# A tuned two-block transformer kernel: the second feed-forward's up projection as block products with seven multiplications

## The chip, the cores and the metric

One core of a Trainium2 chip runs the whole program in one launch. The metric is the device time of that launch in microseconds. The engines meant below are TensorE (PE), VectorE (DVE), ScalarE (ACT), GpSimd (POOL) and SyncE (SP), which here only issues DMAs.

## The reference

Two transformer blocks over 1024 positions of width 1024, one after the other, in float32. The change touches the feed-forward of the second block:

```
u   = rms_norm_2(h, norm_mlp_pre)                # (1024 positions, 1024)
hid = square(relu(u @ w_up))                     # w_up: (1024, 4096)
m   = hid @ w_down                               # w_down: (4096, 1024)
h   = h + rms_norm_2(m, norm_mlp_post)
```

Everything else (the mixers of both blocks and the first feed-forward) is computed as before.

## The kernel before, in words

Activations lie with channels on the partitions and positions along the row: eight tiles of 128 channels by 1024 positions. Every large product is made of float32r matmuls of 128x128 weights on 128x512 positions. To keep float32 accuracy each operand is split into a high part and a low remainder, and three matmuls make one product: high by high, high by low, low by high (L1320 to L1322, in `mm`).

A weight panel is 128x1024 (512 KB). SP loads it into one of two raw buffers (`wraw`, `load`, L2949). ACT copies it with rounding into the high half of one of four slots (`whl`, NW = 4; the ACT `split`, L2408 is the helper's line), POOL subtracts to get the low half (the POOL `split`, L2847). A panel of w_up (`f2u`) covers 128 hidden channels and all 1024 input channels: 8 input tiles x 3 matmuls x 2 halves of the positions = 48 matmuls, in two PSUM tiles of 24. A panel of w_down (`f2d`) covers four hidden tiles and two output tiles, again 48 matmuls, in four PSUM tiles of 12.

The second feed-forward takes 32 f2u panels and 8 chunks of 4 f2d panels, and alternates: after six up panels, four down panels, four up panels, and so on (`ffn`, `ffn_order`). The last chunk's first half of positions is finished for all outputs before its second half, so that its panels come twice. For an up panel ACT evicts the two PSUM tiles with a Relu into `rl`, DVE squares the 128x1024 (`rl<-rl`), ACT writes the high half and POOL the low half of the hidden tile (`hid`); three of the first six low halves are made on DVE. Hidden tiles stay on the chip. For a down tile DVE adds the PSUM tile into `y` (`y<-y,ps`).

The order of the work is one list of steps, written by a planner (`Plan`, `plan.seq`); each engine walks that list and takes the steps that it has code for. So the queues are in order, and a step that waits holds everything that the same engine has behind it. Waits are on semaphores that `mark` and `done` name: `hi` and `lo` for the halves of a panel, `gemm` for a PSUM tile.

## Time and profile before

| | |
|---|---|
| device time, three runs | 2922.83, 2915.71, 2922.82 us (median 2922.82) |
| profiled execution, span | 2914.0 us (the page gives no other time of its own for it) |
| PE busy | 2752.9 us, 94% of the span |
| DVE, ACT, POOL busy | 1347.0, 871.3, 887.3 us |
| second feed-forward, last 700 us of the span | PE busy in all of it from 2250 to 2860 us |
| DMA | 246.47 MB, mean 85 GB/s |

The page gives the busy time of each engine, the chain of work that ended last, the costliest groups of instructions and the DMA issues. A row of a timeline has the start and the duration of an instruction in microseconds, its engine, its line, what it writes and reads, and in brackets how long its engine had been idle and who released it. A matmul's printed duration overlaps with the next one's, so that the pace of PE is read from starts. Where work on DVE, ACT, POOL or SP lies beside PE's, only its lateness counts.

### The profile page before, as it was taken

Reading aid. Unit: us, or ns where it says so; the run is one execution under the profiler, and the core shown is the slowest. Engines: PE = TensorE matmul, PEld = TensorE weight load, DVE = VectorE, ACT = ScalarE, POOL = GpSimd, SP = SyncE. Lnnn points to the kernel's source line nnn. Section 1 sums busy time; section 2 is a strip of 40 time slices with the busy share of each in tenths; the row PEclk is TensorE's granted clock in tenths of the full one; section 3 lists DMA queues with packets and bytes.
Section 4 is the critical chain, followed back from the end, with each engine's and each line's share of the span. In section 5 each row is a group of like instructions: output and inputs, shape, how many; then the busy total and the mean of one; then the engine's idle time right before and its main releaser. Section 6 shows DMA issues by size and latency. Waiting matters only on the chain.

```text
span 2914.0 us, 30872 instructions
## 1 busy us (share of the span) xinstructions
PE 2752.9 (94%) x12774; PEld 2145.0 (74%) x12774; DVE 1347.0 (46%) x1666; ACT 871.3 (30%) x1306; POOL 887.3 (30%) x410
## 2 busy tenths in 40 slices
PE   6888898799999999979999999999999999999997
PEld 3656666678888888767777777677677888888885
DVE  5646668775435453565757522322566212111116
ACT  4313563432212121234454221111344111222112
POOL 1422124243333342344211111111245333333234
PEclk8999999899999999989999999999999999999998
DMA  6453246211111111223112211111323111111113
GB/s 233 175 139 100 75 169 254 101 58 51 51 44 51 51 44 49 101 82 130 44 65 102 65 65 54 64 52 48 130 87 112 55 51 51 44 51 44 51 51 137
DMA packets 86571, 246.47 MB, mean 85 GB/s; under 512 B 10784, under 2 KB 25632, under 8 KB 86432
## 3 DMA queue, kind: packets, MB, share of 16 engines
q1 hardware_dynamic: 78400, 219.77, 22.1%
q10 hardware_dynamic: 4608, 14.92, 1.3%
q0 software_dynamic: 3424, 9.81, 0.9%
q8 instruction: 101, 1.65, 0.2%
q14 instruction: 38, 0.31, 0.0%
HBM read 207.40 MB, written 37.07 MB: 84 GB/s over the span
## 4 chain that ended last, share of the span: by engine, by line
PE 82%; DVE 10%; ACT 3%; issue 2%; DMA 2%; POOL 1%; SPq 0%; ACTq 0%; POOLq 0%; DVEq 0%
PE ps L1320 24%; PE ps L1322 23%; PE ps L1321 23%; PE pc L1667 3%; DVE x L1721 1%; PE pss L1617 1%; PE ps L1480 1%; PE ps L1534 1%; DMA adaw<-in_w_ada 1%; DVE pad L1691 1%; DVE pad L1685 1%; ACT act L2408 1%; PE ps L1499 1%; PE pss L1467 1%; POOL whl L2847 1%
## 5 line engine op out<-in xcount | busy, mean ns | idle before, releaser
L2847 POOL TENSOR_TENSOR whl<-wraw,whl 128x1024 fp32r<-128x1024 f32 (+1 forms) x247 | 645.2, 2614 | 1590.7 <-ACT whl L2408 1590.6
L1320 PE MATMUL ps<-act,whl 128*128 128x512 f32 x2464 | 998.2, 405 | 49.9 <-DVE act L1685 18.0
L1322 PE MATMUL ps<-act,whl 128*128 128x512 f32 x2464 | 974.0, 395 | 0.0
L1321 PE MATMUL ps<-act,whl 128*128 128x512 f32 x2464 | 973.9, 395 | 0.0
L1320 PEld LDWEIGHTS ps<-act,whl 128*128 128x128 f32 x2464 | 469.3, 190 | 183.2 <-issue 69.5
L1321 PEld LDWEIGHTS ps<-act,whl 128*128 128x128 f32 x2464 | 469.7, 191 | 105.5 <-issue 8.2
L1322 PEld LDWEIGHTS ps<-act,whl 128*128 128x128 f32 x2464 | 468.8, 190 | 103.3
L2408 ACT ACTIVATE whl<-wraw 128x1024 fp32r<-128x1024 f32 (+1 forms) x247 | 256.5, 1039 | 446.1 <-PE ps L1322 388.8
L1320 PE MATMUL ps<-hid,whl 128*128 128x512 f32 x864 | 340.4, 394 | 3.8 <-POOL hid L2847 2.1
L1322 PE MATMUL ps<-hid,whl 128*128 128x512 f32 x864 | 337.7, 391 | 0.0
L1321 PE MATMUL ps<-hid,whl 128*128 128x512 f32 x864 | 337.5, 391 | 0.0
L1685 DVE TENSOR_TENSOR y<-y,ps 128x512 f32<-128x512 f32 x176 | 120.4, 687 | 302.0 <-PE ps L1322 301.6
L1320 PEld LDWEIGHTS ps<-hid,whl 128*128 128x128 f32 x864 | 162.5, 188 | 39.5 <-POOL hid L2847 2.9
L1322 PEld LDWEIGHTS ps<-hid,whl 128*128 128x128 f32 x864 | 162.3, 188 | 36.4
L1321 PEld LDWEIGHTS ps<-hid,whl 128*128 128x128 f32 x864 | 162.4, 188 | 35.0 <-issue 0.5
L1685 DVE TENSOR_TENSOR rl<-rl 128x1024 f32<-128x1024 f32 x32 | 44.1, 1378 | 278.1 <-ACT rl L2408 278.1
L2408 ACT ACTIVATE sgm<-ps 128x512 f32<-128x512 f32 x46 | 27.5, 598 | 294.3 <-PE ps L1322 285.9
L1685 DVE TENSOR_TENSOR sgm<-sgm,pc 128x512 f32<-128x512 f32 x48 | 32.7, 682 | 156.3 <-PE pc L1667 156.1
L1667 PE MATMUL pc<-hz,wb 128*128 128x512 f32 x224 | 102.2, 595 | 0.4
L1691 DVE SCALAR_TENSOR_TENSOR cv<-pad,par,cv 128x1024 f32<-128x1024 f32 x44 | 100.0, 2273 | 1.6
L1691 DVE SCALAR_TENSOR_TENSOR pad<-pad,par 128x1024 f32<-128x1024 f32 x44 | 100.0, 2273 | 1.6
L2408 ACT ACTIVATE rl<-ps 128x512 f32<-128x512 f32 x61 | 36.4, 597 | 214.2 <-PE ps L1322 214.2
(312 smaller groups left out, 2471.6 us busy)
## 6 DMA issues: line engine op xcount, KB each, us to landing
wraw<-in_w_in SPq DMA_DIRECT2D x63, 512.0 KB, 3.3
wraw<-in_f1u SPq DMA_DIRECT2D x47, 512.0 KB, 3.2
wraw<-in_f2d SPq DMA_DIRECT2D x36, 512.0 KB, 3.2
wraw<-in_f2u SPq DMA_DIRECT2D x35, 512.0 KB, 3.2
wraw<-in_w_out SPq DMA_DIRECT2D x32, 512.0 KB, 3.3
x<-in_w_ada SPq DMA_DIRECT2D x32, 512.0 KB, 6.1
xs<-y SPq DMA_DIRECT2D x24, 512.0 KB, 7.4
x<-in_xT ACTq DMA_DIRECT2D x16, 512.0 KB, 9.4
```

The lines of the kernel that those rows point to most:

```text
L1320: pe.matmul(PSB[g.bank][:, :], hi, src[:, 0, k, c], start=e == 0, stop=False)
L1321: pe.matmul(PSB[g.bank][:, :], hi, src[:, 1, k, c], start=False, stop=False)
L1322: m = pe.matmul(PSB[g.bank][:, :], lo, src[:, 0, k, c], start=False, stop=e == len(ks) - 1)
L1467: pe.matmul(PSS[:, g, 0:hi - lo], qT[pr, i, n * 128:n * 128 + 128], kT[pr, kc], start=True, stop=True).then_inc(*mark("att", "score", u, g))
L1480: m = pe.matmul(PSB[tb][:, s * 128:s * 128 + 128], scb[u % 3][:, g, s * 128:s * 128 + 128], dgs[u % 2][:, g, :], start=True, stop=True)
L1499: m = pe.matmul(o, vrow[:, blk, 64 * g:64 * g + 64], pts[g][:, s * 128:s * 128 + 128], start=s == 0, stop=s == nb - 1)
L1534: m = pe.matmul(PSB[2 * i + pr][:, :], FA[tp][:, pr, i * 128:i * 128 + 128], dft[tp % 4][:, i * 512:i * 512 + 512], start=tp == 0, stop=tp ...
L1667: m = pe.matmul(PSC[half][:, :], wb[n % 4][:, e, :], YB[2 * k + e][:, HALF[half]], start=e == 0, stop=e == 1)
L1685: return v.tensor_tensor(out, a, b, op)
L1691: return v.scalar_tensor_tensor(out=out, in0=a, scalar=s, in1=b, op0=op0, op1=op1)
L2408: return a.activation(out, in_, func, **kw)
L2847: return g_.tensor_tensor(out, a, b, op)
```

## The change

The up panels 6 to 31 are taken in 13 pairs (units). The weights of a pair are a block matrix of 2x2 quarters: a11 and a12 are the first and second 512 input channels of the pair's first panel, a21 and a22 those of its second. The activations are 2x2 too: b11, b12 (first 512 channels, first and second half of the positions), b21, b22. Instead of eight products of quarters there are seven, by sums on both sides:

- weights: s1 = a21 + a22, s2 = s1 - a11, s3 = a11 - a21, s4 = a12 - s2
- activations, once for all pairs: t1 = b12 - b11, t3 = b22 - b12, t2 = b22 - t1, t4 = b21 - t2
- products, in order, with their PSUM bank: a11 b11 (0), a12 b21 (1), s2 t2 (0), s1 t1 (2), s3 t3 (0), s4 b22 (2), a22 t4 (0)

Each product is 4 input tiles x 3 matmuls = 12 matmuls into a 128x512 bank. The sums of products are made in PSUM, by going on in a bank that has been read but not cleared, and by adds of an evicted bank to another. ACT evicts after products 0, 2, 3 and 6 (counted from 0), DVE adds after 1, 4 and 5 (`pair_ev`); then ACT applies Relu (`pair_hid`) and DVE squares.

s3 and s1 are computed on POOL, s2 and s4 on DVE (`pair_sum`). s1 overwrites a21 in its raw buffer. Every one of the seven weight operands is split on ACT and POOL into a half slot of 512 columns (`pair_split`), six products ahead of PE (`LEAD`). The raw quarters are loaded by SP as 256 KB each (`pair_load`).

Hidden tiles are no longer kept on the chip: SP stores each squared tile to DRAM (`hscr`), except tiles 6, 7 and 8, and loads it back for the down stage (`hid_load`), which now follows as one stretch of 8 chunks after all up work; there ACT and POOL split it (`hid_split`), four hidden tiles beside the chunk before. The rows of w_down are put into the matching order on the host's side of the layout. The normalised activations are written in place into `x` (`norm_tiles`), since the t sums read them.

The names `before3`, `t12`, `t3` lay the new tiles over memory that is free by then; `d_as`, `d_at` and `d_dft` semaphores are renamed and shared with the new loads.

The core of the diff:

```diff
--- before.py
+++ after.py
@@ -140,6 +140,25 @@
+QUARTERS = ("a11", "a12", "a21", "a22")
+PRODUCTS = [("a11", "b11", 0), ("a12", "b21", 1), ("s2", "t2", 0), ("s1", "t1", 2), ("s3", "t3", 0), ("s4", "b22", 2), ("a22", "t4", 0)]
+OPENS = (0, 1, 3)
+PAIRS = {"f2": 13}
+HEAD = 6
+PREFILL = 3
+LEAD = 6
+SIZES = {"f2": [4] * 8}
+ORDER = {"f2": [6, 7, 8] + list(range(6)) + list(range(9, 32))}
...
+            u, k = divmod(m, 7)
+            h = (p.first_op[name] + m) % (2 * NW)
+            p.had_slot[name, m] = p.half_slot[h]
+            p.half_slot[h] = ("pair", name, u, k)
+            if k == 2:
+                for a in ("s3", "s1", "s2"):
+                    p.put("pair_sum", name, u, a)
+            elif k == 4:
+                p.put("pair_sum", name, u, "s4")
+            p.put("pair_split", name, u, k)
+            if u + 1 < units:
+                for q in {3: (0,), 4: (2,), 6: (1, 3)}.get(k, ()):
+                    p.put("pair_load", name, u + 1, q)
...
+        def parts():
+            for t in ("t1", "t3", "t2", "t4"):
+                for e in range(4):
+                    p.put("part_sum", s, t, e)
+                    if t != "t4":
+                        p.put("part_split", s, t, e)
+                    if low:
+                        p.put("part_low", *low)
+                    low = (s, t, e) if t != "t4" else None
+                    yield 1.4
...
+            p.pe(2.73, "pair_mm", name, u, k)
+            prep(m + LEAD)
+            if u == units - 1 and k == 6:
+                p.put("hid_split", name, PREFILL)
+            p.put("pair_ev", name, u, k)
+            if k == 6:
+                for q in range(2):
+                    p.put("pair_hid", name, u, q)
+            if (u, k) in ((1, 1), (1, 3), (2, 1)):
+                p.put("hid_split", name, k // 2 if u == 1 else 2)
...
@@ -978,8 +1162,10 @@
+    p.limit = STREAM.index(("f2d", 0))
     pre = finish(out_proj("w_out2", 4), 4, "f2u", (0, 1, 2))
-    ffn("f2", 32, 5, p.gemm("f2u", range(32), 3, pre), hidden2, None, ())
+    pairs("f2", 4, p.gemm("f2u", range(HEAD), 3, pre), HEAD)
+    chunks_down("f2", 5, None, ())
...
@@ PE: pair_mm
+            def pair_mm(name, u, k):
+                s, (a, b, bank) = PAIR_S[name], PRODUCTS[k]
+                o = pair_banks(u)[bank]
+                w.wait_ge(*done("pairH", name, u, k))
+                w.wait_ge(*done("pairL", name, u, k))
...
+                elif k == 2:
+                    w.wait_ge(*done("pairA", name, u, 0))
+                elif k == 4:
+                    w.wait_ge(*done("pairA", name, u, 2))
+                elif k == 5:
+                    w.wait_ge(*done("pairA", name, u, 3))
+                else:
+                    w.wait_ge(*done("pairD", name, u, 4))
...
+                    pe.matmul(o[:, :], hi[:, c], x_hi, start=k in OPENS and e == 0, stop=False, skip_group_check=True)
+                    pe.matmul(o[:, :], hi[:, c], x_lo, start=False, stop=False, skip_group_check=True)
+                    m = pe.matmul(o[:, :], lo[:, c], x_hi, start=False, stop=e == 3, skip_group_check=True)
+                m.then_inc(*mark("pairM", name, u, k))
...
@@ DVE
+            def pair_sum(name, u, a):
+                a11, a12, a21, a22 = (wraw[:, n // 2, 512 * (n % 2):512 * (n % 2) + 512] for n in range(4))
+                t3, t2 = stemp[name]
+                if a in ("s3", "s1"):
+                    return
+                if a == "s2":
+                    w.wait_ge(*done("pairL", name, u, "s1"))
+                    if u:
+                        w.wait_ge(*done("pairL", name, u - 1, 5))
+                    m = tt(t2, a21, a11, ALU.subtract)
+                else:
+                    w.wait_ge(*done("d_q1", name, u))
+                    w.wait_ge(*done("pairL", name, u, 2))
+                    m = tt(t2, a12, t2, ALU.subtract)
+                m.then_inc(*mark("pairS", name, u, a))
+            def pair_ev(name, u, k):
+                bank = pair_banks(u)[PRODUCTS[k][2]]
+                xa, xb = pair_tiles(name, u)[1]
+                if k in (1, 4, 5):
+                    o, first = {1: (xa[:, 0:512], 0), 4: (xb[:, 512:1024], 3), 5: (xa[:, 512:1024], 2)}[k]
+                    w.wait_ge(*done("pairM", name, u, k))
+                    w.wait_ge(*done("pairA", name, u, first))
+                    tt(o, o, bank[:, :], ALU.add).then_inc(*mark("pairD", name, u, k))
+            def pair_hid(name, u, q):
+                i, x = (v_[q] for v_ in pair_tiles(name, u))
+                w.wait_ge(*done("pairA", name, u, "relu", q))
+                tt(x, x, x, ALU.mult).then_inc(*mark("h2D", i))
...
@@ ACT
+            def pair_split(name, u, k):
+                a = PRODUCTS[k][0]
+                if a in QUARTERS:
+                    w.wait_ge(*done(f"d_q{QUARTERS.index(a)}", name, u))
+                else:
+                    w.wait_ge(*done("pairL" if a in ("s3", "s1") else "pairS", name, u, a))
+                w.wait_ge(*op_free(name, u, k))
+                av(pair_op(name, u, k)[:, 0, :], pair_raw(name, k), ACT.Copy).then_inc(*mark("pairH", name, u, k))
+            def pair_ev(name, u, k):
+                bank = pair_banks(u)[PRODUCTS[k][2]]
+                xa, xb = pair_tiles(name, u)[1]
+                if k in (0, 2, 3, 6):
+                    o = {0: xa[:, 0:512], 2: xa[:, 512:1024], 3: xb[:, 512:1024], 6: xb[:, 0:512]}[k]
+                    w.wait_ge(*done("pairM", name, u, k))
+                    if k in (0, 3):
+                        free = tile_free(name, u, int(k == 3))
+                        if free:
+                            w.wait_ge(*free)
+                        else:
+                            for e in range(4):
+                                w.wait_ge(*part_lo(PAIR_S[name], "t3", e))
+                    av(o, bank[:, :], ACT.Relu if k == 6 else ACT.Copy).then_inc(*mark("pairA", name, u, k))
+            def pair_hid(name, u, q):
+                i, x = (v_[q] for v_ in pair_tiles(name, u))
+                w.wait_ge(*done("pairD", name, u, 4 if q else 5))
+                if q:
+                    x = x[:, 512:1024]
+                av(x, x, ACT.Relu).then_inc(*mark("pairA", name, u, "relu", q))
...
@@ POOL
+            def pair_sum(name, u, a):
+                if a == "s3":
+                    w.wait_ge(*done("d_q0", name, u))
+                    w.wait_ge(*done("d_q2", name, u))
+                    if u:
+                        w.wait_ge(*done("pairL", name, u - 1, 4))
+                    tt(stemp[name][0], a11, a21, ALU.subtract).then_inc(*mark("pairL", name, u, "s3"))
+                elif a == "s1":
+                    w.wait_ge(*done("d_q3", name, u))
+                    w.wait_ge(*done("pairL", name, u, "s3"))
+                    tt(a21, a21, a22, ALU.add).then_inc(*mark("pairL", name, u, "s1"))
+            def pair_split(name, u, k):
+                w.wait_ge(*done("pairH", name, u, k))
+                hi, lo = (pair_op(name, u, k)[:, q, :] for q in range(2))
+                tt(lo, pair_raw(name, k), hi.bitcast(F32), ALU.subtract).then_inc(*mark("pairL", name, u, k))
+            def hid_split(name, h):
+                w.wait_ge(*done("hidA", name, h))
+                tt(hid_view(name, 1, h), hid_raw(name, h), hid_view(name, 0, h).bitcast(F32), ALU.subtract).then_inc(
+                    *mark("hidP", name, h))
...
@@ SP
+            def pair_load(name, u, c):
+                if u:
+                    w.wait_ge(*done("pairL", name, u - 1, (0, 1, 3, 6)[c]))
+                    w.wait_ge(*(done("pairL", name, u - 1, "s1") if c == 3 else done("pairS", name, u - 1, ("s2", "s4", "s2")[c])))
+                else:
+                    w.wait_ge(*done("lo", plan.limit_of[name] - 1))
+                    w.wait_ge(*done("lo", plan.limit_of[name] - 2))
+                h = 512 * (c % 2)
+                q.dma_start(wraw[:, c // 2, h:h + 512], t[name + "u"][HEAD + 2 * u + c // 2, :, h:h + 512]).then_inc(
+                    *dmark(f"d_q{c}", name, u))
+            def h2(i):
+                w.wait_ge(*done("h2D", i))
+                b = store_ring(i)
+                q.dma_start(t["hscr"][i], rl[b][:, :]).then_inc(*dmark(f"d_h{b}", "f2", i))
+            def pair_hid(name, u, e):
+                i, x = (v_[e] for v_ in pair_tiles(name, u))
+                if not kept(name, i):
+                    w.wait_ge(*done("h2D", i))
+                    q.dma_start(t["hscr"][i], x).then_inc(*dmark(f"d_h{store_ring(i)}", name, i))
+            def hid_load(name, h):
...
+                w.wait_ge(*done(f"d_h{store_ring(i)}", name, i))
+                q.dma_start(hid_raw(name, h), t["hscr"][i]).then_inc(*dmark(f"d_hl{h % 7}", name, h))```

What stands on ACT in the middle of the up stage before: two evictions to an up panel, the split of a weight panel, the high half of a hidden tile.

```order
L2408 ACTIVATE whl<-wraw 128x1024 [waits gemm,d_w0]
L2408 ACTIVATE rl<-ps 128x512 [waits hidP,gemm]
L2408 ACTIVATE rl<-ps 128x512 [waits gemm]
L2408 ACTIVATE whl<-wraw 128x1024 [waits d_w1]
L2408 ACTIVATE hid<-rl 128x1024 [waits h2D]
```

ACT in the changed kernel, from the split of operand 6 of one unit (a22) over a whole unit. `rl<-ps` and `x<-ps` are evictions, after products 0, 2, 3 and 6; `whl<-wraw` and `whl<-ss` are splits for the unit after, in the order a11, a12, s2, s1, s3, s4; `d_q0` to `d_q3` are the loads of the four quarters.

```order
L2785 ACTIVATE whl<-wraw 128x512 [waits d_q3]
L2785 ACTIVATE rl<-ps 128x512 [waits hidP,pairM]
L2785 ACTIVATE whl<-wraw 128x512 [waits d_q0]
L2785 ACTIVATE whl<-wraw 128x512 [waits d_q1]
L2785 ACTIVATE rl<-ps 128x512 [waits pairM]
L2785 ACTIVATE whl<-ss 128x512 [waits pairS]
L2785 ACTIVATE x<-ps 128x512 [waits d_h3,pairM]
L2785 ACTIVATE whl<-wraw 128x512 [waits pairL]
L2785 ACTIVATE whl<-ss 128x512
L2785 ACTIVATE whl<-ss 128x512 [waits pairM,pairS]
L2785 ACTIVATE x<-ps 128x512 [waits pairM]
L2785 ACTIVATE rl<-rl 128x1024 [waits pairD]
```

The evictions now stand between splits that wait for loads and for sums on other engines: the split of a12 (waits `d_q1`) is ahead of the eviction of product 2, and the split of s2 (waits `pairS`) is ahead of the eviction of product 3.

POOL in one unit of the changed kernel: the low halves of a22, of the next unit's a11 and a12, the sums s3 and s1, and the low halves of s2, s1, s3, s4.

```order
L3272 TENSOR_TENSOR whl<-wraw,whl 128x512 [waits pairH] x3
L3272 TENSOR_TENSOR ss<-wraw 128x512 [waits pairL,d_q2,d_q0]
L3272 TENSOR_TENSOR wraw<-wraw 128x512 [waits pairL,d_q3]
L3272 TENSOR_TENSOR whl<-ss,whl 128x512 [waits pairH]
L3272 TENSOR_TENSOR whl<-wraw,whl 128x512 [waits pairH]
L3272 TENSOR_TENSOR whl<-ss,whl 128x512 [waits pairH] x2
```

Before, POOL had one 128x1024 low half for a weight panel and one for a hidden tile. Now the two sums stand behind the low half of a12.

SP in the changed kernel, one unit (the stores of both hidden tiles; loads of a12, a22, and of the next a11 and a21, in this order):

```order
L3426 DMA hscr<-rl 128x1024 [waits h2D] x2
L3414 DMA wraw<-in_f2u 128x512 [waits pairS]
L3414 DMA wraw<-in_f2u 128x512 [waits pairL]
L3414 DMA wraw<-in_f2u 128x512 [waits pairS,pairL]
L3414 DMA wraw<-in_f2u 128x512 [waits pairL]
```

Before, SP had here only panel loads, each waiting for the low half of the panel two before it. Now the loads of a12 and a22 stand behind two stores, which wait for the squares (`h2D`).

## Rows read from the trace of the kernel before

**Rows 1.** Busy time of each engine, from the page.
```profile
PE 2752.9 (94%) x12774; PEld 2145.0 (74%) x12774; DVE 1347.0 (46%) x1666; ACT 871.3 (30%) x1306; POOL 887.3 (30%) x410
```

**Rows 2.** Stretches: length, busy time (instructions) of PE, PEld, DVE, ACT, POOL; clock; DMA.
```profile
2400.00:2500.00 100.00, 100.00 (x439) 82.14 (x438) 17.14 (x21) 20.29 (x24) 35.06 (x15) 1.00 0.15 51
...
2880.00:2914.00 34.00, 13.99 (x54) 10.18 (x53) 23.48 (x30) 3.24 (x6) 14.43 (x11) 0.70 0.32 124
```

**Rows 3.** PE's waits from 2800 us on: total, times, longest.
```profile
PE pc L1289 <- DVE ss L1685: 3.4, 1, 3.4
PE pc L1554 <- DVE rl L1685: 1.3, 1, 1.3
PE ps L1320 <- POOL hid L2847: 0.5, 1, 0.5
```

**Rows 4.** ACT's timeline in the feed-forward: start, duration, instruction, idle before.
```profile
2300.74 0.60 ACT L2408 ACTIVATE rl<-ps 128x512 f32<-128x512 f32 x1 [4.33 <-PE ps L1322]
2306.18 0.60 ACT L2408 ACTIVATE rl<-ps 128x512 f32<-128x512 f32 x1 [4.84 <-PE ps L1322]
2306.67 1.05 ACT L2408 ACTIVATE whl<-wraw 128x1024 fp32r<-128x1024 f32 x1
...
2394.43 1.05 ACT L2408 ACTIVATE whl<-wraw 128x1024 fp32r<-128x1024 f32 x1
```

**Rows 5.** PE's timeline where a PSUM tile ends.
```profile
2300.32 0.39 PE L1322 MATMUL ps<-act,whl 128*128 128x512 f32 x1
2300.54 0.39 PE L1320 MATMUL ps<-act,whl 128*128 128x512 f32 x1
```

**Rows 6.** DVE's timeline around the stage's start.
```profile
2203.39 3.22 DVE L1685 TENSOR_TENSOR ss<-ss,sq 128x512 f32<-128x512 f32 x3
...
2221.79 0.69 DVE L1685 TENSOR_TENSOR act<-tm,act 128x512 fp32r<-128x512 f32 x1
...
2238.56 2.22 DVE L1685 TENSOR_TENSOR hid<-rl,hid 128x1024 fp32r<-128x1024 f32 x1 [1.12 <-ACT hid L2408]
2240.70 3.41 DVE L1685 TENSOR_TENSOR rl<-rl 128x1024 f32<-128x1024 f32 x1
2306.88 1.23 DVE L1685 TENSOR_TENSOR rl<-rl 128x1024 f32<-128x1024 f32 x1 [10.90 <-ACT rl L2408]
```

**Rows 7.** POOL's timeline at the same places.
```profile
2218.39 1.30 POOL L2847 TENSOR_TENSOR act<-tm,act 128x512 fp32r<-128x512 f32 x1 [0.75 <-ACT act L2408]
2236.31 3.39 POOL L2847 TENSOR_TENSOR hid<-rl,hid 128x1024 fp32r<-128x1024 f32 x1
2239.65 6.73 POOL L2847 TENSOR_TENSOR whl<-wraw,whl 128x1024 fp32r<-128x1024 f32 x2
...
2307.80 2.56 POOL L2847 TENSOR_TENSOR whl<-wraw,whl 128x1024 fp32r<-128x1024 f32 x1 [8.93 <-ACT whl L2408]
2310.33 2.39 POOL L2847 TENSOR_TENSOR hid<-rl,hid 128x1024 fp32r<-128x1024 f32 x1
```

**Rows 8.** Groups of 2300 to 2800 us: count | busy us, mean ns | idle before.
```profile
L1685 DVE TENSOR_TENSOR y<-y,ps 128x512 f32<-128x512 f32 x88 | 60.6, 689 | 173.3 <-PE ps L1322 173.3
```

**Rows 9.** DMA issues: tile and source, queue, count, KB each, median us to landing.
```profile
wraw<-in_f2u SPq DMA_DIRECT2D x35, 512.0 KB, 3.2
xs<-y SPq DMA_DIRECT2D x24, 512.0 KB, 7.4
out_T<-y SPq DMA_DIRECT2D x12, 256.0 KB, 2.0
yb<-z SPq DMA_DIRECT2D x5, 512.0 KB, 2.6
```

**Rows 10.** DMA issues in 1655 to 1665 us, where a store follows a load at once.
```profile
wraw<-in_w_in SPq DMA_DIRECT2D x1, 512.0 KB, 4.4
gs<-gt SPq DMA_DIRECT2D x1, 512.0 KB, 5.5
```

**Rows 11.** SP's timeline there: start and duration of each issue.
```profile
1656.38 0.33 SPq L2949 DMA_DIRECT2D wraw<-in_w_in  x1
1656.76 0.43 SPq L3132 DMA_DIRECT2D gs<-gt  x1
```

More of the change, by code:

```diff
@@ L779, in ffn, with pairs, prep, behind @@
         return finish(down_last, s, kind, idxs)
+    def pairs(name, s, seq, hidden):
+        kind, units = name + "u", PAIRS[name]
+        total = 7 * units
+        nxt = p.limit
+        p.first_op[name] = 2 * ((nxt + p.shift) % NW)
+        p.limit_of[name] = nxt
+        sent = [0]
+        def prep(m):
+            if m >= total:
+                return
[12 more added lines that the diff above has]
+                    p.put("pair_load", name, u + 1, q)
+        def behind(n):
+            if p.splits == nxt and sent[0] == 0:
+                for q in range(4):
+                    p.put("pair_load", name, 0, q)
+                sent[0] = 1
+            if p.splits == nxt and n >= nxt - 3:
+                for _ in range(2):
+                    if sent[0] - 1 < LEAD:
+                        prep(sent[0] - 1)
+                        sent[0] += 1
+        def parts():
+            low = None
+            for t in ("t1", "t3", "t2", "t4"):
[7 more added lines that the diff above has]
+                    yield 1.4
+        p.on_limit = behind
+        p.beside(parts(), 4.0)
+        for i in range(hidden):
+            until_tile(seq)
+            p.put("h2", i)
+        p.on_limit = None
+        p.settle()
+        for e in range(4):
+            p.put("part_split", s, "t4", e)
+        for e in range(4):
+            p.put("part_low", s, "t4", e)
+        for m in range(sent[0] - 1, LEAD):
+            prep(m)
+        p.pair_hold[name] = [p.hold[b] for b in range(4)]
+        opened = 0
+        for m in range(total):
+            u, k = divmod(m, 7)
+            if m + LEAD >= total and p.limit == nxt:
+                p.limit = len(STREAM)
+                p.raw_of = {nxt: (name, units - 1), nxt + 1: (name, units - 1)}
+                p.shift += ((p.first_op[name] + total + 1) // 2 - nxt - p.shift) % NW
+                p.load()
+                p.load()
+            p.pe(2.73, "pair_mm", name, u, k)
[8 more added lines that the diff above has]
+                p.put("hid_split", name, k // 2 if u == 1 else 2)
+            if u == units - 1 and k == 4:
+                p.put("hid_load", name, PREFILL)
+            while p.limit > nxt and opened < NW and all(
+                    h is None or h[0] == "panel" and h[1] < nxt or h[0] == "pair" and h[2] * 7 + h[3] <= m - 1
+                    for h in p.half_slot[2 * ((p.splits + p.shift) % NW):][:2]):
+                p.split()
+                opened += 1
+        p.hold.update({0: ("pairA", name, units - 2, 6), 1: ("pairD", name, units - 2, 1), 2: ("pairD", name, units - 2, 5), 3: ("pairA", name, units - 1, 6)})
@@ L1178, in build, with norm_tiles @@
         RES_DST = {1: t["xs"], 2: t["xs2"], 4: t["xs"], 5: t["out"]}
+        def norm_tiles(s, half):
+            if s in PAIR_S.values():
+                return [X[s][:, j, HALF[half]] for j in range(8)]
+            return TMP[s]
         def rb_bank(s, half):
@@ new lines, in whl_free, with op_free, hid_raw @@
+        def whl_free(n):
+            out = []
+            for h in plan.had_slot[n]:
+                if h and h[0] == "panel":
+                    out.append(done("gemm", plan.done_tile[h[1]]))
+                elif h:
+                    out.append(done("pairM", *h[1:]))
+            return out
+        def op_free(name, u, k):
+            h = plan.had_slot[name, 7 * u + k]
+            return done("gemm", plan.done_tile[h[1]]) if h[0] == "panel" else done("pairM", *h[1:])
+        def hid_raw(name, h):
+            if h < PREFILL:
+                return xring[name][(ORDER[name][h] - HEAD) % 4]
+            return hid_view(name, 1, h).bitcast(F32)
@@ L1187, in build, with part_lo @@
+        def part_lo(s, t, e):
+            return done("pairL", s, t, e) if t in ("t1", "t3") else done("pairS", s, t, e, "lo")
         last_up = {"f1": 21, "f2": 31}
```

330 lines of the change are left out of this document (267 added, 63 removed).

## The prediction

> **What bounds the kernel now.** I read the page's busy times first: PE is busy for 94% of the span, no other engine for half of it [rows 1]. Then the stretches: from 2400 to 2500 us, in the feed-forward that is changed, PE is busy in all of it at full clock, with DVE, ACT and POOL at 17, 20 and 35 of 100 us; only the last 34 us, the closing norm, have PE idle for 20 us [rows 2]. Then PE's waits: none between 2300 and 2800 us, and from 2800 us on only one of 0.5 us in matmul work, the others belong to the closing norm [rows 3]. So the stage costs its number of matmuls times their pace, and nothing else. The pace comes from ACT's panel splits, which PE's progress releases: from 2306.67 to 2394.43 us lie eight panels of 48 matmuls [rows 4], 87.76 / 384 = 0.2285 us for one.
>
> **What the change removes.** Two up panels had 96 matmuls, a unit has 7 x 12 = 84. Thirteen units save 156 matmuls: 156 x 0.2285 = 35.6 us. The down stage keeps its matmuls. This is the whole possible gain, and it comes only if PE stays fed. A product takes 12 x 0.2285 = 2.74 us, a unit 19.19 us.
>
> **Is there enough engine time in a unit?** POOL has seven low halves and two sums of 128x512. Such an instruction takes 1.30 us [rows 7], nine take 11.7 us. ACT has seven splits and four evictions at 0.60 us (128x512 [rows 4]), a Relu of 1024 at 1.05 and one of 512: 8.3 us. DVE has three adds from PSUM at 0.69 [rows 8], two sums of 512 at 0.69 [rows 6] and two squares at 1.23 [rows 6]: 5.9 us. DMA moves 1 MB of weights and 1 MB of stores in 19.2 us, about 109 GB/s. All fit. What doesn't follow from sums is the order.
>
> **POOL and DVE hold each other up.** The square of a 1024-wide tile takes 1.23 us alone, and 3.41 at 2240.70, while POOL had started an instruction at 2239.65 [rows 6, 7]. POOL's own low half takes 2.39 alone and 3.39 there. Both numbers are those of turns: a 2.4 us instruction of POOL, then some 1.1 us of DVE, then POOL again. The adds of a PSUM tile don't show it: 88 of them have a mean of 0.689 beside a POOL that works a third of the time [rows 8]. The Trainium skill, page "SBUF — State Buffer", section "SBUF: two separate sides", says this of the shared pair: an exclusive lock for a whole instruction, taken on DVE's side also by operations with two inputs in SBUF. The trace agrees. By it POOL and DVE together need 11.7 + 2 x 1.23 + 2 x 0.69 = 15.5 of 19.19 us: still room, but every turn lengthens a chain.
>
> **The chain that closes on itself.** I follow one unit from the end of its last product (time 0; PE goes straight into the next unit).
> 1. ACT evicts product 6: starts 0.2 after the tile's end (2300.54 to 2300.74 [rows 4, 5]). Its next instruction starts 0.49 later, though the one before takes 0.60 (2306.18 to 2306.67 [rows 4]). Relu of the first tile 0.69 to 1.75, of the second to 2.25, then the split of a22 to 2.75.
> 2. DVE squares the first tile from 1.83 to 3.06. POOL, released at 2.83 for the low half of a22, comes next in the turns, to 4.3. The second square follows, to about 5.4.
> 3. SP stands at the store of the second tile until then. Only behind it come the loads of a12 and a22 for the unit after next: store at 5.45, load of a12 at about 5.95 (0.43 an issue and a gap [rows 11]).
> 4. Its landing is not in the trace in this form. Bounds: 256 KB take 2.0 us where nothing else moves (a store to the output [rows 9]), which gives 8.0. A load and a store of 512 KB issued 0.38 apart land after 4.4 and 5.5, the last 5.9 from the first issue, where one alone takes 3.2 or 2.6 [rows 9 to 11]; so each further 512 KB puts some 2.6 us on top. For the store alone 2.6, plus half of 2.6 for 256 KB, plus 0.2: 4.1 from 5.45, or 9.5. I take 9.5. The far end is the burst of eight stores, median 7.4 for one [rows 9]: 5.95 + 7.4 = 13.3.
> 5. From the landing: ACT splits a12 (0.1 + 0.6). POOL makes its low half, then s3, then s1, as its queue has them: 3 x 1.27 = 3.8. DVE makes s2 (0.1 + 0.69), ACT splits it (0.1, and 0.5 to its next start), and only behind that split stands the eviction of product 3 of the running unit (0.60, and 0.15 to PE). Sum 6.65: it is out at 9.5 + 6.65 = 16.15.
> 6. PE needs that eviction before product 5, which goes on in the same bank. Product 5 would start at 5 x 2.74 = 13.71. PE waits 16.15 - 13.71 = 2.4 us.
>
> After it come products 5 and 6, and the chain starts anew, so the wait doesn't heal. It needs a unit whose tile is stored (units 1 to 12) and weights still to be loaded for two units later (units 0 to 10): ten times, 24.4 us. By the bounds of step 4: at 8.0 the wait is 0.9; if besides the second square goes ahead of POOL (done at 4.2, landing 6.8) it is nothing; at 13.3 it is 6.2. So 0 to 62 us.
>
> **Other terms.** The t sums (16 subtractions on DVE, 16 splits on ACT, eight low halves each on POOL and DVE) lie beside the six head panels, 6 x 10.97 us of PE. There they take 24 x 0.69 = 16.6 us of DVE and 8 x 1.3 = 10.4 of POOL, while 7 us of hidden low halves leave DVE and 7 us POOL; panels are four slots ahead. If evictions come late behind part splits it costs some us: -1 to 4. At the seam to the units, ACT has four t4 splits ahead of the first eviction, 2.4 us inside a product; at the seam to the down stage hidden tile 9 must be loaded (3.2) and split (1.05 + 2.39) within products 5 and 6 and three quarters of the first tile, 7.5 us against 6.7. Together I take 1 us. In the down stage, POOL has one panel and one hidden tile for 10.97 us of PE: 2 x 2.39 [rows 7] = 4.8, ACT 2.1; loads are a chunk ahead. Nothing. The tail is as before, less the wait of 0.5 [rows 3]; that I leave out.
>
> **Sum.** -35.6 + 24.4 + 1 = -10.2 us, against the profiled execution's 2914.0, thus 2903.8. The median of the three runs is 8.8 above that span (another is 1.7 above); with the same distance the changed kernel takes 2912.6. I say 2912.
>
> **Rivals.**
> - *All hidden.* DVE gets its second square ahead of POOL, and the load lands in 2.5 us: step 6 gives less than 1 us. For it: 2.0 for 256 KB [rows 9]. Against it: POOL got its turn first at 2240.70 [rows 6, 7], and a load with a store beside it took 4.4 where one alone takes 3.2 [rows 9, 10]. At half a us each, 35.6 - 1 - 5 = 29.6 is gained: 2893; at best 2888.
> - *The load can't land before the store.* As a mechanism here: the load's completion comes no earlier than that of the store ahead, which with traffic beside it took 5.5 [rows 10]: 5.45 + 5.5 = 10.95, wait 3.9, ten times 39 us: +4 us, 2927, within the bound of no change. Speaking for it is that the store is issued first here; against it, that a store alone lands in 2.6 [rows 9]. The Trainium skill, page "DMA: Bandwidth & Descriptors", section "Queues, rings and completion order", states such a rule: the semaphore's increment lands only after all earlier writes of that DMA engine. No row here isolates it.
> - *Slower.* The same place, but the loads land as in the burst of stores: 7.4 after issue, wait 6.2, 62 us, total 35.6 gained and 63 lost: 2950. The balance tips to slower than before at a wait of 3.5 a unit, a landing at 10.5, and beyond the bound of measurement at 4.3, a landing at 11.4. For it: a store of 512 KB took 7.4 in the median [rows 9]. Against it: those were eight in a row, here there are two in 19 us.
> - *The stage is starved elsewhere*, at the seams or since a hidden tile comes late in each chunk: 8 chunks x 1 us, 2920.
>
> **How the numbers follow.** Forecast 0.53, all hidden 0.17, store ahead 0.14, slower 0.08, starved elsewhere 0.08. What a measurement of this kernel can tell from no change is about 0.3%, 8.8 us: faster is below 2914, slower above 2931.6. The forecast's own range is 2902 to 2922 (waits of 1.4 to 3.4 a unit), and a little over half of it lies below 2914: 0.31. With all of the hidden case and a fifth of the starved one: faster 0.50. Slower: its own 0.08, a quarter of the store case: 0.12. The rest, 0.38, is no change. For 8 in 10 the range goes from 2890 to 2930.
>
> **What would show it.** PE should have 156 matmuls fewer. Between the head panels and the down stage there should be ten waits of PE at a product on the tile t or act, on ACT, of 2 to 3 us each, one in a unit, and a period of 21.6 us where a unit of work is 19.2. ACT should wait in each unit for the load of a12 and for DVE's `ss`. Squares of 2.2 or more beside POOL, and loads of 256 KB landing after 3.5 us, would bear out steps 2 and 4. The forecast is wrong if units follow at 19.2 us, if PE waits at another product, or if PE waits for POOL's low halves themselves, which by this working are six products ahead.

## The result: slower by 0.7%, and the profile after

The changed kernel takes 2942.08 us (median of four runs, 2940.07 to 2945.4) against 2922.82 of the kernel before (2915.71 to 2924.95). The ratio is 1.0073, with a 95% interval of 1.0055 to 1.009. I had forecast 2912, with a range up to 2930. The profiled execution has a span of 2938.3 us, 24.3 more than before.

The page after, answering to [rows 1]: PE's busy time fell by 13 us only, while 156 matmuls are gone; DVE and POOL have 92 and 114 us more.

```profile
span 2938.3 us, 31088 instructions
PE 2739.5 (93%) x12618; PEld 2125.2 (72%) x12618; DVE 1438.5 (49%) x1752; ACT 920.2 (31%) x1413; POOL 1001.7 (34%) x512
```

PE's waits from 2150 us on, answering to [rows 3]: engine, line, who was waited for, us in total, times, longest.

```profile
PE ps L1646 <- ACT x L2785: 12.2, 6, 2.6
PE pc L1646 <- ACT rl L2785: 11.7, 5, 2.4
PE ps L1646 <- ACT rl L2785: 7.2, 1, 7.2
PE ps L1612 <- DVE act L2010: 6.8, 2, 4.5
PE ps L1646 <- DVE act L2010: 4.8, 1, 4.8
...
PE ps L1612 <- POOL hid L3272: 0.9, 1, 0.9
```

L1646 is the first of the three matmuls that `pair_mm` issues for an input tile. The first two rows are eleven waits in the units, alternating between two sets of banks. The third and the fifth are at the head seam, from the six head panels to the units; the last is at the down seam, from the units to the down stage; the rest belongs to the norms and was there before. The stretches, answering to [rows 2] (length, busy us of PE, PEld, DVE, ACT, POOL, granted clock, DMA share, GB/s), show something else beside the waits:

```profile
2250.00:2300.00 50.00, 38.02 (x149) 30.27 (x148) 30.63 (x28) 19.58 (x34) 34.48 (x23) 0.86 0.22 75
2300.00:2400.00 100.00, 90.02 (x360) 71.34 (x359) 34.36 (x32) 34.98 (x59) 62.38 (x43) 0.93 0.24 84
2400.00:2500.00 100.00, 90.33 (x372) 72.54 (x371) 34.71 (x30) 34.13 (x58) 54.11 (x38) 0.95 0.26 90
...
2700.00:2800.00 100.00, 100.00 (x439) 82.13 (x438) 25.13 (x37) 18.08 (x18) 42.92 (x18) 1.00 0.30 107
```

The granted clock fell to 0.86, 0.93 and 0.95 where the waits are. A hundred microseconds hold 360 matmuls there; 90 us of busy time would hold 394 at the old pace. PE's timeline behind one wait shows it:

```profile
2394.97 0.47 PE L1646 MATMUL ps<-act,whl 128*128 128x512 f32 x1 [2.21 <-ACT x L2785]
...
2396.88 0.63 PE L1647 MATMUL ps<-act,whl 128*128 128x512 f32 x1
2397.30 0.63 PE L1648 MATMUL ps<-act,whl 128*128 128x512 f32 x1
```

After a wait of 2.2 us PE runs for 1.5 us at the old pace, then starts come 0.43 us apart until 2399.85. The granted clock of that stretch is 0.50, the lower of PE's two levels (1.2 GHz):

```profile
2396.50:2399.80 3.30, 3.30 (x9) 2.59 (x8) 1.55 (x2) 0.63 (x1) 3.30 (x3) 0.50 0.23 79
```

From 2225 to 2570 us, 83 matmuls have 0.35 us or more to the next start, 0.427 as a rule: 83 x (0.427 - 0.2285) = 16.5 us. 19 of them are at the head seam (3.8 us), 64 in the units (12.7 us).

**Where 24.3 us come from**, read from starts on PE: -35.6 for the matmuls, +25.7 for eleven waits in the units (ten of 2.3 to 2.8, one of 1.0; a wait counted beyond the normal distance of two starts), +12.3 at the head seam (7.38 and 4.91), +16.5 slow matmuls, +0.5 at the down seam (1.1, where the kernel before waited for 0.6), +1.1 that the stage starts later already. That is 20.5. Of the remaining 3.8, 2.2 lie in the down stage: its 1536 matmuls take 355.0 us without that wait, the last 1536 of the kernel before 352.8. I didn't look for its cause.

### The profile page after: what moved, and what is told of

Its sections match the earlier page's. It is cut to its first block, busy times and chain, and to the rows that moved or that the text cites. A ratio compares the mean times of both kernels' runs of the same rounds, so it can differ in the third digit from the quotient of the medians.

```text
span 2938.3 us, 31088 instructions
## 1 busy us (share of the span) xinstructions
PE 2739.5 (93%) x12618; PEld 2125.2 (72%) x12618; DVE 1438.5 (49%) x1752; ACT 920.2 (31%) x1413; POOL 1001.7 (34%) x512
## 4 chain that ended last, share of the span: by engine, by line
PE 75%; DVE 11%; POOL 4%; issue 4%; ACT 3%; DMA 3%; SPq 0%; ACTq 0%; POOLq 0%; DVEq 0%
PE ps L1612 20%; PE ps L1613 20%; PE ps L1614 20%; PE pc L1992 3%; POOL whl L3272 2%; DVE x L2046 1%; PE pss L1942 1%; PE ps L1805 1%; PE ps L1859 1%; DVE ss L2010 1%; PE ps L1646 1%; ACT rl L2785 1%; DMA adaw<-in_w_ada 1%; PE ps L1647 1%; PE ps L1648 1%
## 5 line engine op out<-in xcount | busy, mean ns | idle before, releaser
L3272 POOL TENSOR_TENSOR whl<-wraw,whl 128x1024 fp32r<-128x1024 f32 (+2 forms) x273 | 653.1, 2396 | 1462.9 <-ACT whl L2785 1462.7
L1612 PE MATMUL ps<-act,whl 128*128 128x512 f32 x2240 | 910.9, 407 | 50.6 <-DVE act L2010 18.0
L1613 PE MATMUL ps<-act,whl 128*128 128x512 f32 x2240 | 885.5, 395 | 0.0
L1614 PE MATMUL ps<-act,whl 128*128 128x512 f32 x2240 | 885.2, 395 | 0.0
L1612 PEld LDWEIGHTS ps<-act,whl 128*128 128x128 f32 x2240 | 426.6, 190 | 175.4 <-issue 70.0
L1613 PEld LDWEIGHTS ps<-act,whl 128*128 128x128 f32 x2240 | 427.2, 191 | 96.9 <-issue 8.2
L1614 PEld LDWEIGHTS ps<-act,whl 128*128 128x128 f32 x2240 | 426.5, 190 | 95.5
L2785 ACT ACTIVATE whl<-wraw 128x1024 fp32r<-128x1024 f32 (+2 forms) x273 | 261.2, 959 | 479.3 <-PE ps L1614 362.0
L2010 DVE TENSOR_TENSOR y<-y,ps 128x512 f32<-128x512 f32 x176 | 120.3, 687 | 311.0 <-PE ps L1614 310.7
L1612 PE MATMUL ps<-hid,whl 128*128 128x512 f32 x672 | 264.8, 394 | 4.2 <-POOL hid L3272 2.5
L1613 PE MATMUL ps<-hid,whl 128*128 128x512 f32 x672 | 263.2, 392 | 0.0
L1614 PE MATMUL ps<-hid,whl 128*128 128x512 f32 x672 | 262.3, 390 | 0.0
L1612 PEld LDWEIGHTS ps<-hid,whl 128*128 128x128 f32 x672 | 126.2, 188 | 33.5 <-POOL hid L3272 3.4
L1614 PEld LDWEIGHTS ps<-hid,whl 128*128 128x128 f32 x672 | 126.2, 188 | 28.3
L1613 PEld LDWEIGHTS ps<-hid,whl 128*128 128x128 f32 x672 | 126.2, 188 | 27.2 <-issue 0.5
L2785 ACT ACTIVATE sgm<-ps 128x512 f32<-128x512 f32 x46 | 27.5, 597 | 294.2 <-PE ps L1614 286.0
L2010 DVE TENSOR_TENSOR sgm<-sgm,pc 128x512 f32<-128x512 f32 x48 | 32.7, 682 | 156.3 <-PE pc L1992 156.1
L2010 DVE TENSOR_TENSOR ss<-ss,sq 128x512 f32<-128x512 f32 x70 | 80.3, 1156 | 25.0 <-ACT sq L2785 24.4
L2785 ACT ACTIVATE pad<-ps 128x512 f32<-128x512 f32 x85 | 49.6, 590 | 120.4 <-PE ps L1614 120.4
## 6 DMA issues: line engine op xcount, KB each, us to landing
wraw<-in_w_in SPq DMA_DIRECT2D x63, 512.0 KB, 3.3
wraw<-in_f1u SPq DMA_DIRECT2D x47, 512.0 KB, 3.2
wraw<-in_f2d SPq DMA_DIRECT2D x36, 512.0 KB, 3.3
wraw<-in_w_out SPq DMA_DIRECT2D x32, 512.0 KB, 3.4
x<-in_w_ada SPq DMA_DIRECT2D x32, 512.0 KB, 5.9
wraw<-in_f2u SPq DMA_DIRECT2D x52, 256.0 KB, 3.1
xs<-y SPq DMA_DIRECT2D x24, 512.0 KB, 6.8
hscr<-rl SPq DMA_DIRECT2D x23, 512.0 KB, 2.6
```

The costliest lines, as they stand in the source:

```text
L1612: pe.matmul(PSB[g.bank][:, :], hi, x_hi, start=e == 0, stop=False)
L1613: pe.matmul(PSB[g.bank][:, :], hi, x_lo, start=False, stop=False)
L1614: m = pe.matmul(PSB[g.bank][:, :], lo, x_hi, start=False, stop=e == len(ks) - 1)
L2010: return v.tensor_tensor(out, a, b, op)
L2785: return a.activation(out, in_, func, **kw)
L3272: return g_.tensor_tensor(out, a, b, op)
```

## The chain in a unit, predicted and seen

Timelines of one unit, ACT, DVE, SP and POOL (start, duration, instruction, idle before). Its predecessor's last product ended at 2402.15, PE's next start.

```profile
2402.35 0.60 ACT L2785 ACTIVATE x<-ps 128x512 f32<-128x512 f32 x1 [4.18 <-PE ps L1648]
...
2411.76 0.63 ACT L2785 ACTIVATE whl<-wraw 128x512 fp32r<-128x512 f32 x1 [5.58 <-DMA wraw<-in_f2u]
2412.30 0.58 ACT L2785 ACTIVATE rl<-ps 128x512 f32<-128x512 f32 x1
2417.20 0.63 ACT L2785 ACTIVATE whl<-ss 128x512 fp32r<-128x512 f32 x1 [4.32 <-DVE ss L2010]
2417.74 0.58 ACT L2785 ACTIVATE rl<-pc 128x512 f32<-128x512 f32 x1
```
```profile
2403.93 1.22 DVE L2010 TENSOR_TENSOR rl<-rl 128x1024 f32<-128x1024 f32 x1 [3.99 <-ACT rl L2785]
2405.07 2.32 DVE L2010 TENSOR_TENSOR x<-x 128x1024 f32<-128x1024 f32 x1
...
2416.48 0.69 DVE L2010 TENSOR_TENSOR ss<-wraw 128x512 f32<-128x512 f32 x1 [8.00 <-POOL wraw L3272]
```
```profile
2407.41 0.33 SPq L3426 DMA_DIRECT2D hscr<-x  x1
2407.78 13.03 SPq L3414 DMA_DIRECT2D wraw<-in_f2u  x4
```
```profile
2412.47 1.29 POOL L3272 TENSOR_TENSOR whl<-wraw,whl 128x512 fp32r<-128x512 f32 x1 [3.94 <-ACT whl L2785]
2413.72 1.30 POOL L3272 TENSOR_TENSOR ss<-wraw 128x512 f32<-128x512 f32 x1
2415.16 1.28 POOL L3272 TENSOR_TENSOR wraw<-wraw 128x512 f32<-128x512 f32 x1
```

Counted from 2402.15, predicted and measured: second square done 5.4 and 5.2; load of a12 issued 5.95 and 5.6; a12 there 9.5 and 9.6; s2 started 14.1 and 14.3; eviction of product 3 out, PE goes on, 16.15 and 16.3 (2418.46). The second square took 2.32 us beside a POOL that had work from 2405.01 to 2408.53, as in [rows 6, 7]. The load behind the store took 4.0 us to land; that of the store was 2.9.

## The experiments

**The eviction ahead.** The rival was that the operands themselves come late.

```diff
             p.pe(2.73, "pair_mm", name, u, k)
+            p.put("pair_ev", name, u, k)
             prep(m + LEAD)
...
-            p.put("pair_ev", name, u, k)
```

> The eviction of each product is put ahead of the preparation of the operand six products on, on every engine; nothing else is changed. Theory (the eviction of product 3 stands on ACT behind the split of s2): the eleven waits of 2.3 to 2.8 us at product 5, 25.7 us in all, go, since the split of s2 is then only ahead of the eviction of product 6, 5.5 us later. If the slow matmuls behind each wait are a consequence of the wait, they go too, some 12 us more: about 2942 - 25.7 - 12 = 2904. Rival 1 (the slow matmuls come from the busier engines, not from the waits): waits gone, granted clock in the units still 0.92 to 0.95, 2916. Rival 2 (the operands themselves are late): the waits move to another product and the time stays near 2942. The waits at the seam, 12.3 us, stay by every theory.

2904.95 us, ratio to before 0.9938 (0.9917 to 0.9958). PE's waits in 2215 to 2620 us, and a stretch in the units:

```profile
PE ps L1646 <- ACT rl L2785: 7.2, 1, 7.2
PE ps L1646 <- DVE act L2010: 4.5, 1, 4.5
PE ps L1612 <- DVE act L2010: 2.3, 1, 2.3
PE ps L1612 <- POOL hid L3272: 2.0, 1, 2.0
```
```profile
2290.00:2400.00 110.00, 110.00 (x481) 90.02 (x481) 38.45 (x40) 46.76 (x77) 79.13 (x54) 1.00 0.28 98
```

All waits in the units are gone, and the granted clock there is 1.00 while POOL is at least as busy as in the changed kernel (79 of 110 us; there 62 of 100): the slow matmuls followed from the waits, not from the busy engines. 18 slow matmuls (3.6 us) are left at the head seam and none in the units. Rival 1 and rival 2 fall. The five runs lie apart, three at 2905 to 2907 us and two at 2896 to 2897, so that what a later kernel gains on the median of this one is better read from the table at the end of this section. The down seam's wait grew from 0.9 to 2.0, since the late hidden tile's split now stands behind the last eviction.

**The load ahead of the stores.**

```diff
-                for q in {3: (0,), 4: (2,), 6: (1, 3)}.get(k, ()):
+                for q in {3: (0,), 4: (2,), 5: (1,), 6: (3,)}.get(k, ()):
```

> The load of a12 is issued one product earlier, so that it stands ahead of the two stores in SP's queue; the order on ACT stays. Theory (step 3 of the prediction, the loads stand behind the stores): the low half of a12 and s3 are done early, the chain then starts at the landing of a22, about 9.3 after the unit's start, and only s1, s2, the split and the eviction follow: 12.7 against 13.7 needed, so waits fall from 2.4 to under 0.5 us a unit: 2904 to 2910. Rival (the store isn't what matters, POOL's three instructions and DVE's are): the waits fall by less than a half: above 2925.

2904.79 us, 0.995 (0.9935 to 0.9965). PE's waits in the units are down to two of 1.0 us (0.9 in the profile's count), in the first units:

```profile
PE ps L1646 <- ACT x L2785: 0.9, 1, 0.9
PE pc L1646 <- ACT rl L2785: 0.9, 1, 0.9
```

So the order on SP alone is enough too: the theory holds, and the rival falls.

**All weight sums on DVE.** s3 and s1 move from POOL's `pair_sum` to DVE's, with the same waits; order and loads are those of the changed kernel.

```diff
+                if a == "s3":
+                    ...
+                    m = tt(t3, a11, a21, ALU.subtract)
+                elif a == "s1":
+                    ...
+                    m = tt(a21, a21, a22, ALU.add)
```

> All four weight sums on DVE instead of two on GpSimd, order and loads as in the changed kernel. Theory (POOL's two sums are 2.7 us of the chain): they leave the queue behind the low half of a12, and take 0.7 us each on DVE; a22's landing (about 10.3) then starts s1, s2, split, eviction: about 12.9 to 13.5 against 13.7: waits under 0.5 us, and about 2906. The a12 split still is ahead of the eviction of product 2, which costs nothing below a landing at 9.6 and a few tenths above. Rival (the shared turns of DVE and POOL make DVE as slow as POOL was, 1.7 us a sum): waits of 1 to 2 us stay, 2925 to 2935.

2902.61 us, 0.9943 (0.9928 to 0.9958). No wait in the units from 2290 us on. DVE's groups in 2290 to 2530 us, then s1 and s2 of one unit:

```profile
L2010 DVE TENSOR_TENSOR ss<-wraw 128x512 f32<-128x512 f32 x22 | 26.0, 1180 | 0.4
L2010 DVE TENSOR_TENSOR ss<-wraw,ss 128x512 f32<-128x512 f32 x11 | 18.5, 1684 | 0.1
...
2415.67 0.69 DVE L2010 TENSOR_TENSOR wraw<-wraw 128x512 f32<-128x512 f32 x1 [2.98 <-DMA wraw<-in_f2u]
2416.40 1.67 DVE L2010 TENSOR_TENSOR ss<-wraw 128x512 f32<-128x512 f32 x1
```

The rival was right in its mechanism, even on the chain: s2 takes 1.67 us in every unit and s4 1.5 to 2.1, since POOL is at a low half beside them, while s3 and all but the first s1 take 0.7 (the mean of 1180 ns mixes s3 and s2). It was wrong in its result: s1 and s2 take 2.4 us together, where POOL's three instructions and s2 took 4.7 in the changed kernel. The eviction of product 3 ends at 2419.22 in that unit, and PE goes on at 2419.40, where product 5 was due: the wait is gone with at most 0.2 us to spare.

**Both edits of order.**

> Both edits, the eviction ahead and the load of a12 ahead of the stores. Theory: either alone takes away the waits in the units, so that both together are no faster than the first alone, within 2 us: 2902 to 2906; what is left over the ideal are the seam's 12.3 us and its slow matmuls. Rival: if each takes away only a part, the two together are faster than each alone by 5 us or more.

2903.31 us, 0.995 (0.9932 to 0.9967), no faster than either alone. Three different cuts of one chain give the same time, within 2.5 us in the table below: it was one chain, and each of the three cuts gives nearly all of it back.

**The seam: turns or order?** The kernel of e1_ev_first with the t sums 8 columns wide:

```diff
-                    m = tt(b11, b12, b11, ALU.subtract)
+                    m = tt(b11[:, 0:8], b12[:, 0:8], b11[:, 0:8], ALU.subtract)
...
```

> The kernel of e1_ev_first with the 16 t sums on DVE narrowed from 512 to 8 columns, so that the t operands hold other values and the output isn't the reference's; every instruction, wait and queue place stays. Theory A (the head lacks turns: DVE's and POOL's instructions with two inputs in SBUF exclude each other, and from 2223 to 2259 they would need 16 x 0.69 + 8 x 0.69 + 6 x 1.23 + 2 x 0.69 on DVE and 8 x 1.3 + 3 x 2.4 + 8 x 1.3 on POOL, some 53 us): taking out about 10 us of DVE gives back most of the seam's 7.4 and 4.6 us of waits and its slow matmuls: 2904.9 - 12 = 2893, waits at the seam under 3 us in all. Theory B (only the order on ACT holds the evictions up): the waits stay above 8 us, since every wait is still there, 2900 or more.

The kernel leaves out the other 504 columns of each sum, so its output isn't the reference's. 2894.99 us, 0.9911 (0.9896 to 0.9926), 10 less than the median of e1_ev_first, of which 7.0 lie in the stage (table below). DVE is busy for 22.5 us from 2223 to 2259, instead of 29.0 in the changed kernel, whose stage starts at nearly the same time (2217.6, here 2217.8), and the waits at the seam fall to 5.3 in the profile's count:

```profile
PE ps L1646 <- DVE act L2010: 2.8, 1, 2.8
PE ps L1646 <- POOL wraw L3272: 2.5, 1, 2.5
```

Every wait and place in a queue is still there, so DVE's time and not the order alone made the seam: 6.4 of its 12.0 us in e1_ev_first. Under 3 us were expected to be left, and 5.7 are, counted on PE's starts. Two rows say why it may not be less: two 8-column subtractions take 0.24 us together where POOL is idle, and one takes 1.25 us beside a POOL instruction.

```profile
2244.69 0.24 DVE L2010 TENSOR_TENSOR x<-x 128x8 f32<-128x8 f32 x2
...
2250.39 1.25 DVE L2010 TENSOR_TENSOR x<-x 128x8 f32<-128x8 f32 x1
```

**The seam in another order.** The kernel of e1_ev_first with three t2 splits behind the last head evictions, the t4 splits and low halves behind the first product's eviction:

```diff
-                    yield 1.4
+                    yield 2.6
...
-        for e in range(4):
-            p.put("part_split", s, "t4", e)
-        for e in range(4):
-            p.put("part_low", s, "t4", e)
...
+            if m == 0:
+                for e in range(4):
+                    p.put("part_split", s, "t4", e)
+                for e in range(4):
+                    p.put("part_low", s, "t4", e)
             prep(m + LEAD)
```

> The kernel of e1_ev_first with another order at the seam: the t steps are spread wider (2.6 instead of 1.4 us of the planner's time) so that three t2 splits no longer stand on ACT ahead of the last head evictions, and the t4 splits and low halves come behind the eviction of the first product. Theory A (turns): the first wait gets shorter but product 2, which needs t2's low halves, waits instead; the sum of the seam's waits stays near 12 us, at best 9, and the time within 4 us of e1_ev_first. Theory B (order): the first wait of 7.4 falls below 3 and the second of 4.6 below 2, 2896 or less.

2902.07 us, 0.9934 (0.9918 to 0.9951). That is 2.9 less than the median of e1_ev_first, but between the ends of the stage both take the same (658.0 and 658.1, table below). There are 11.8 us of waits at the seam, where e1_ev_first has 11.7, now most of it in one wait of 9.6:

```profile
PE ps L1647 <- ACT rl L2786: 11.3, 2, 9.6
```

Order moves the wait and doesn't remove it, as theory A has it.

**Both at the seam: that order with all sums on DVE.**

> The kernel of e8_seam_order with all four weight sums on DVE. In the units nothing waits any more with either engine making the sums, so the two should be within 2 us of each other; at the seam POOL has two instructions of 1.7 us fewer and DVE two of 0.7 to 1.7 more, in turns: a gain of 1 to 2 us. Rival: DVE, which is the longer queue at the seam, gets later, 2 us slower.

2898.01 us, 0.992 (0.9905 to 0.9935): 4.1 less than e8_seam_order (3.5 in the stage) where 1 to 2 were expected. The long wait fell from 9.6 to 7.6. The direction was right, the size too small. That each turn of POOL less saves DVE's wait behind it as well would explain it; it isn't shown.

**More room: eight head panels, twelve pairs.** The kernel of e1_ev_first with:

```diff
-PAIRS = {"f2": 13}
-HEAD = 6
+PAIRS = {"f2": 12}
+HEAD = 8
...
-ORDER = {"f2": [6, 7, 8] + list(range(6)) + list(range(9, 32))}
+ORDER = {"f2": [8, 9, 10] + list(range(8)) + list(range(11, 32))}
...
```

> The kernel of e1_ev_first with eight head panels and twelve pairs instead of six and thirteen: 12 matmuls more (2.7 us), and 21.9 us more of PE beside the same t work. Theory A (turns): the need of some 60 us has 21.9 us more to lie beside, so that the seam's 12 us of waits and about 5 us of slow matmuls nearly go: 2904.9 + 2.7 - 14 = 2894. Theory B (order on ACT at the seam, whatever the room): the t splits are long done when the last evictions come, so that the waits go too, and this run doesn't tell the two apart; it is here for its time. If the waits stay as they are, neither theory holds: 2908.

2891.57 us, 0.9903 (0.9888 to 0.9917): 13.4 less than the median of e1_ev_first, 9.5 in the stage, though PE has 12 matmuls more. There is no wait at the head seam, and the clock is full in a stretch where e1_ev_first had 0.83:

```profile
2250.00:2290.00 40.00, 40.00 (x177) 32.88 (x176) 33.45 (x26) 17.63 (x32) 25.67 (x15) 1.00 0.41 150
```

**The best of these together** (eight head panels, evictions ahead, sums on DVE), with this order, in which the split of the late hidden tile stands ahead of the last eviction:

```diff
-            prep(m + LEAD)
             if u == units - 1 and k == 6:
                 p.put("hid_split", name, PREFILL)
             p.put("pair_ev", name, u, k)
+            prep(m + LEAD)
```

> Eight head panels and twelve pairs, the evictions ahead of the preparations, all four weight sums on DVE, and at the seam to the down stage the split of the late hidden tile ahead of the last eviction, as in the changed kernel. e6_head8 took 2891.6 with 3.1 us of wait at the down seam, 2.7 us of slow matmuls behind it and 1.6 at product 6 of the last unit. If these waits are the ACT order at the last product (the hidden tile's split came behind the eviction), the down seam's wait falls to about 1 us as in the changed kernel, and its slow matmuls go: 2891.6 - 4 = 2888. If the sums on DVE matter at the head still, 1 us less; if the balance of turns in the head has become easy, nothing more.

A second kernel has the diff of e2_load_first as well:

> As e9_head8_dve with the load of a12 ahead of the stores too. No wait in the units is left that it could shorten: within 2 us of e9_head8_dve, 2886 to 2890. If it is faster by more, some wait in the units that I put down as gone was left.

2892.13 us, 0.9903 (0.9886 to 0.992), and 2889.8 us, 0.9896 (0.9877 to 0.9915). They are the same as e6_head8 within what these runs tell, so 1% faster than the kernel before and 1.8% faster than the changed one. What I had expected of the down seam didn't come: it still has 2.7 us of wait for the hidden tile, with the split ahead of the eviction or behind it.

```profile
PE ps L1612 <- POOL hid L3280: 2.7, 1, 2.7
PE ps L1612 <- DVE act L2010: 2.3, 1, 2.3
PE ps L1646 <- ACT rl L2793: 1.4, 1, 1.4
```

e6_head8 had 2.9 there with the split behind the eviction. So that wait isn't the ACT order at the last product. ACT waits there for the tile's load from DRAM, as the timelines of ACT and SP in e9_head8_dve show:

```profile
2508.70 1.06 ACT L2793 ACTIVATE hid<-hid 128x1024 fp32r<-128x1024 f32 x1 [3.51 <-DMA hid<-hscr]
```
```profile
2503.20 0.33 SPq L3399 DMA_DIRECT2D wraw<-in_f2d  x1
2503.94 0.33 SPq L3436 DMA_DIRECT2D hid<-hscr  x1
```

The load is issued 2.1 us after product 5 of the last unit started (2501.81), behind that of a panel, and lands 4.7 later; the split and POOL's low half follow, and PE goes on at 2512.2. In the changed kernel it is issued 0.6 us after product 5 started and lands 4.4 later. e6_head8 and e10_loads_too have the 2.1 as well. What holds the panel's load isn't shown.

**The stage alone.** What lies ahead of the stage takes up to 8.8 us more in one profiled execution than in another, though no experiment changes it: PE's last wait ahead of the t sums, for the normalised activations (2.91 us between two starts), ends between 2217.0 and 2225.8 us. Kernels are therefore compared here from the end of that wait to the start of the last matmul of the down stage, one profiled execution of each:

| kernel | us |
|---|---|
| before; changed | 673.2; 696.9 |
| e1_ev_first, e2_load_first, e3_sums_dve, e12_both | 658.1, 659.9, 657.4, 658.1 |
| e5_small_t, e8_seam_order, e138_seam_dve | 651.1, 658.0, 654.4 |
| e6_head8, e9_head8_dve, e10_loads_too | 648.6, 646.4, 648.0 |

## Why the prediction was wrong

- **The gain.** 156 matmuls at 0.2285 us: right. e6_head8, with 144 fewer (32.9 us at that pace), is 24.6 us shorter than the kernel before between the ends of the stage.
- **The chain in the unit.** Right in every link, in the place (product 5) and in the size: 24.4 us predicted, 25.7 measured; ten waits of 2.3 to 2.8 us, and one of 1.0 in a unit whose predecessor stores nothing. Of the bounds of step 4 the value taken, 9.5, was met by 9.6. The stores landed after 2.6 to 3.0 us, the loads behind them after 3.7 to 4.4 and so well behind the store. The rule of the Trainium skill, page "DMA: Bandwidth & Descriptors", section "Queues, rings and completion order", that a semaphore's increment lands only after every earlier write of its DMA engine, agrees with this and doesn't decide here.
- **Failed: "If evictions come late behind part splits it costs some us: -1 to 4 ... Together I take 1 us."** The seam cost 12.3 us of waits. I had added the t work up engine by engine, 16.6 us of DVE and 10.4 of POOL, beside 65.8 us of PE, and only for a unit had I added the two engines as turns. Two things were wrong with it. A part of the six panels' first halves is done before the activations of the second half exist: PE had 29 us of head left when the sums could start (2223.5 to 2252.4), not 66. And the turns of both engines, some 53 us by the sum in the expectation of e5_small_t, stood against these 29, of which only 2.0 found both engines without an instruction. e5_small_t shows it for DVE's time: less of it took away 6.4 us of the seam's waits. e8_seam_order fits, since another order moved the waits and left their sum; e6_head8 had more room and no wait at the head seam, but that would come of either theory. What made the 5.7 us that e5_small_t kept isn't shown. The down seam's part was small: the hidden tile's load, issued 0.6 us after product 5 started, took 4.4 us where 3.2 stood in the sum, and PE waited for 1.1. From 2223 to 2275 us the t sums took 1.57 us in the mean instead of 0.69. The rule of the Trainium skill, page "SBUF — State Buffer", section "SBUF: two separate sides", by which such instructions exclude each other, agrees with the trace. The rows are DVE's group, the first t sum, the last matmul of the head and the next one:

```profile
L2010 DVE TENSOR_TENSOR x<-x 128x512 f32<-128x512 f32 x16 | 24.7, 1572 | 0.0
...
2223.52 0.68 DVE L2010 TENSOR_TENSOR x<-x 128x512 f32<-128x512 f32 x1
...
2252.12 0.39 PE L1614 MATMUL ps<-act,whl 128*128 128x512 f32 x1
2259.73 0.77 PE L1646 MATMUL ps<-act,whl 128*128 128x512 f32 x1 [7.22 <-ACT rl L2785]
```

- **Failed too: a term that the sum put at nothing without a reason, what a wait does to the clock.** It had no term for the matmuls behind a wait. Eight of the ten waits of 2.3 to 2.8 us between 2325 and 2535, and both at the seam, were followed by matmuls at 0.43 us, eight in the mean: 16.5 us, two thirds of the span's excess over the kernel before. e1_ev_first took the waits in the units away and the slow matmuls there went with them. The rows shown of before had a hint, a clock of 0.70 in the last 34 us [rows 2], and its timeline has eight such matmuls around 2219 us, behind a wait of 2.3 us; two of its rows stand below. With the two terms, -35.6 + 25.7 + 12.3 + 16.5 = +18.9; the forecast was -10.2.

```profile
2216.48 0.47 PE L1320 MATMUL ps<-act,whl 128*128 128x512 f32 x1 [2.32 <-DVE act L1685]
...
2217.87 0.63 PE L1322 MATMUL ps<-act,whl 128*128 128x512 f32 x1
```

- **The rivals.** "Slower" came, but not by its mechanism: the loads landed after 3.7 to 4.4 us, not 7.4. Of "starved elsewhere" the seam was the true part.

## What to carry to other kernels

Price a short stall at more than its length: here the 25.7 us of waits in the units cost another 12.7 in slow matmuls. Before adding work beside a transition, add up DVE's instructions with two inputs in SBUF and all of POOL's as one queue, and set them against the PE time that is left once their inputs exist. In in-order queues, put what PE waits for (evictions) ahead of what is prepared for later: that alone turned 0.7% slower into 0.6% faster.
